# Second feed-forward projection in one core: high weights against high and low activations in one 512-column product

## Chip, core and metric

The kernel runs on one core of one Trainium2 chip. The metric is the device time of one execution in microseconds (us); lower is better. One execution was also taken by the profiler, and all rows below come from that one.

## What is computed

Two transformer-like blocks, one after the other, on 256 tokens of 1024 features, in float32. Among their parts stand eight gated feed-forward blocks. Each adds half of its result to the residual `x`:

```python
def swiglu_ffn(h, w_in, w_out):
    gate, up = jnp.split(h @ w_in, 2, axis=-1)
    return (jax.nn.silu(gate) * up) @ w_out

x = x + 0.5 * swiglu_ffn(rms_norm(x, ffn1_norm[i]), ffn1_w_in[i], ffn1_w_out[i])
```

`w_in` is 1024 x 5632 and `w_out` 2816 x 1024. Between the feed-forward blocks stand the mixers: a recurrent one (rwkv), a gated chunk mixer (gmlp), two cross attentions, a linear recurrence (hgrn) and a dilated attention (dil). All their projections use the same machinery.

## The kernel before, in words

**Products.** Activations are kept transposed, features on the 128 partitions and the 256 tokens (`T`) along the row. A weight matrix comes as "slabs": 128 output features by 8 chunks of 128 input features (512 KB) or, for `w_out`, by 11 chunks (`WIDE`, 704 KB). TensorE rounds its operands in the fast float32r mode, so each operand is split in two: high part and low part. For each chunk three products are added in one bank of PSUM: high weights by high activations, high weights by low activations, low weights by high activations (L470, L475, L476 in `pe_stage`). Each is a weight load of 128 columns and a matmul of 256 columns.

**The ring.** Slabs pass through a ring of 4 slots (`raw`, `hi`, `lo`). SyncE issues the DMA into `raw`; ScalarE rounds it into `hi` (`act_hi`, L339); VectorE subtracts and gives `lo` (`dve_lo`, L347); TensorE uses it and counts `slab_used`. Each step waits on a counting semaphore of the step before.

**A feed-forward block.** The first projection runs over 22 pairs of slabs, gate and up; ScalarE and VectorE make the activation and split it into `Ah` and `Al` (22 chunks of 256 tokens each). The second projection runs over 8 output tiles (`NC`), each of 2 slabs of 11 chunks, so 66 matmuls a tile and 528 a block. Its tiles alternate between banks 0 and 2, and fill the left 256 of the 512 columns of a bank. Blocks are called ffn0 to ffn7 below. In the first round of the ring one of the 528 is issued as two, of 192 and 64 columns (L473, `parted`); several other stages do this too.

**The residual.** After a tile VectorE adds the bank, times 0.5, to the row block of `X` (L623 in `dve_resid`) and counts `banks_freed`. ScalarE then makes the next norm's high part `Hh` (L561) and the square (L565), VectorE the low part `Hl` (L569) and the sum of squares (L579); both then go on with the two slabs that take the freed slots. In ScalarE's and VectorE's queues this order is fixed by the program.

**The joint to the next stage.** Where the next stage starts from `X`, TensorE begins it with chunks 0 to 6 of its first two slabs (42 matmuls, L451 to L453), which need only tiles 0 to 6, then multiplies the sum of squares by a matrix of ones (L645), then takes chunk 7. Two feed-forward blocks, the first and the fourth, are followed by a part that needs the whole norm first (`UNSPLIT`: the rwkv mixer and the norm between the two blocks); there TensorE issues products of constants (L406) to fill the time. After the last block four DMAs on SyncE's queue store `X` (L3050).

Of the kernel before, what the change touches and what calls it, by code (L numbers as in the profile page):

```python
# [24 lines left out]
F32R = mybir.dt.float32r  # L25
I32 = mybir.dt.int32
ALU = mybir.AluOpType
# [3 lines left out]
P = 128  # L31
T = 256
# [186 lines left out]
class Resources:  # L219


    def __init__(self, nc, ctx, io, counts):
        self.nc, self.io = nc, io

        def sb(name, shape, dt=F32):
            return ctx.enter_context(nc.sbuf_tensor(name, shape, dt))

        def sem(name):
            return ctx.enter_context(nc.semaphore(name))


        self.raw = sb("raw", [P, RING, WIDE * P])
        self.hi = sb("hi", [P, RING, WIDE * P], F32R)
        self.lo = sb("lo", [P, RING, WIDE * P], F32R)
        self.X = sb("X", [P, NC, T])
        self.R = sb("R", [P, T])
        self.STD = sb("STD", [P, T])
        self.SQSUM = sb("SQSUM", [P, T])
        self.SQ = sb("SQ", [P, 2, T])
        self.vec = sb("vec", [P, N_COLS])  # L240
        self.cols = sb("cols", [P, ONE_HOT + 15])
        self.masks = sb("masks", [P, len(MASKS), P])
        self.sel = sb("sel", [P, NC * 16])
        self.base = -(-nc.sbuf_base // 64) * 64
        self.room = nc.sbuf_usable_end - self.base
        self.arena = sb("arena", [P, (self.room - 128) // 4])
        self.limit = self.room - 128


        self.Hh = self.at("Hh", 0, [P, NC, T], F32R)  # L250
        self.Hl = self.at("Hl", 8 * KB, [P, NC, T], F32R)
        self.memk = self.at("memk", 16 * KB, [P, NC, T])
        self.memv = self.at("memv", 24 * KB, [P, 2, D])
        self.Kh = self.at("Kh", 16 * KB, [P, NC, T], F32R)
        self.Kl = self.at("Kl", 24 * KB, [P, NC, T], F32R)
        self.RKV = self.at("RKV", 84 * KB, [P, T])
        self.gate = self.at("gate", 32 * KB, [P, 2, T])
        self.sgate = self.at("sgate", 34 * KB, [P, 2, T])
        self.up = self.at("up", 36 * KB, [P, 2, T])
        self.act32 = self.at("act32", 38 * KB, [P, 2, T])  # L260
        self.A0 = 40 * KB
        self.Ah = self.at("Ah", self.A0, [P, FC, T], F32R)
        self.Al = self.at("Al", self.A0 + 22 * KB, [P, FC, T], F32R)

        self.bank = [ctx.enter_context(nc.psum_tensor(f"bank{b}", [P, 512], F32)) for b in range(8)]

        self.ident, self.ones, self.head_ones = self.mask("identity"), self.mask("ones"), self.mask("head_ones")


        self.landed = [sem(f"slab_landed{q}") for q in range(RING)]  # L270
        self.hi_ready = sem("hi_ready")
        self.lo_ready = sem("lo_ready")
        self.slab_used = sem("slab_used")
        self.banks_freed = sem("banks_freed")
        self.h_hi, self.h_lo = sem("h_hi_ready"), sem("h_lo_ready")
        self.kv_hi, self.kv_lo = sem("kv_hi_ready"), sem("kv_lo_ready")
        self.sq_ready, self.sq_added = sem("square_ready"), sem("square_added")
        self.ss_ready, self.std_ready, self.rstd_ready = sem("sumsq_ready"), sem("std_ready"), sem("rstd_ready")
        self.gate_scaled, self.silu_done = sem("gate_scaled"), sem("silu_done")
        self.a_ready, self.ah_ready, self.al_ready = sem("a_ready"), sem("ah_ready"), sem("al_ready")  # L280
        self.gelu_done = sem("gelu_done")
        self.proj_act = sem("projection_activated")
        self.loaded = sem("small_loads")
        self.masks_loaded = sem("masks_loaded")
        self.x_loaded = [sem(f"x_half{h}_loaded") for h in range(2)]
        self.mem_loaded = [sem(f"mem_half{h}_loaded") for h in range(2)]
        self.x_scaled = sem("x_scaled")
        self.mixer_loads = sem("mixer_loads")
        self.mixer_stores = sem("mixer_stores")
        self.pair_loaded = [sem(f"pair_loaded{q}") for q in range(2)]  # L290
        self.out_stored = sem("out_stored")
        self.pe_done = Steps(sem("mixer_products"), counts.setdefault("mixer_products", {}))
        self.act_done = Steps(sem("mixer_activations"), counts.setdefault("mixer_activations", {}))
        self.dve_done = Steps(sem("mixer_vectors"), counts.setdefault("mixer_vectors", {}))
        self.pool_done = Steps(sem("mixer_pool"), counts.setdefault("mixer_pool", {}))

        self.loads_before = 0
# [20 lines left out]
class Shared:  # L318
# [113 lines left out]
    def pe_stage(self, pe, st, moving, ready, between=None, after_first=None, late=False, rest=False, chunks_first=False, pair=False):  # L432
# [83 lines left out]
        else:  # L516
            body(0, parted=True)
            with pe.Fori(1, st.iters) as i:
                body(i)

    def pe_first_stage(self, pe, st, late=False, pair=False):

        self.split_n["pe"] += NC
        self.pe_stage_h(pe, st, lambda: self.norm(pe, "pe"), late, pair=pair)
# [84 lines left out]
            if gain != "mix_norm0":  # L609
                act.preload_act_table(ACT.Sqrt)  # L610

    def dve_resid(self, dve, st, coef, gain, keys=False):

        k, split = self.k, gain not in UNSPLIT
        late = st.per_tile == 1

        def prepare(c):
            dve.wait_ge(k.banks_freed, RING + st.base + (c + 1) * st.per_tile)
            self.prep(dve, "dve", k.X, gain, c, split)
        for c in range(NC):  # L620
            s = st.base + c * st.per_tile
            dve.wait_ge(k.slab_used, s + st.per_tile)
            dve.scalar_tensor_tensor(k.X[:, c, :], k.bank[s % RING][:, :T], coef, k.X[:, c, :],  # L623
                                     ALU.mult, ALU.add).then_inc(k.banks_freed, st.per_tile)
            if gain and late and c:
                prepare(c - 1)
            if gain and (c == NC - 1 or not late):
                prepare(c)
            if keys and c:
                self.keys_lo(dve, c - 1)  # L630
            for kg in range(st.per_tile):
                w = st.width if s + kg + RING < st.base + st.slabs else st.ahead
                self.dve_lo(dve, s + kg + RING, (s + kg) % RING, w)
        if gain:
            self.prepped("dve", split)
# [33 lines left out]
class FeedForward:  # L669
# [7 lines left out]
    def pe(self, pe):  # L677
        sh, k = self.sh, self.k
        if self.n == 0:
            pe.wait_ge(k.x_loaded[0], 16)  # L680
            sh.pe_keep_awake(pe, 5, k.X[:, 0, :P], k.X[:, 1, :])
        sh.pe_first_stage(pe, self.st_in, late=self.n == 0)
        done = 2 + FC * self.n
        sh.pe_stage(pe, self.st_out,
                    lambda kg, kc: (k.Ah[:, kg * WIDE + kc, :], k.Al[:, kg * WIDE + kc, :]),
                    lambda kg, kc: pe.wait_ge(k.al_ready, done + WIDE * kg + kc + 1))

    def act(self, act):
        sh, k, st = self.sh, self.k, self.st_in
# [20 lines left out]
    def dve(self, dve):  # L710
# [7 lines left out]
        def body(i, ahead):  # L718
            for j in range(2):
                m, s = 2 * i + j, st.base + RING * i + 2 * j  # L720
                g = FC * self.n + m
                dve.wait_ge(k.slab_used, s + 1)
                dve.wait_ge(k.silu_done, g + 1)
                dve.tensor_tensor(k.gate[:, j, :], k.bank[2 * j][:, :T], k.R[:], ALU.mult).then_inc(k.gate_scaled, 1)  # L724
                sh.dve_lo(dve, s + RING, 2 * j, ahead)
                dve.wait_ge(k.slab_used, s + 2)
                dve.wait_ge(k.a_ready, g + 1)
                dve.tensor_tensor(k.up[:, j, :], k.bank[2 * j + 1][:, :T], k.R[:], ALU.mult).then_inc(k.banks_freed, 2)
                dve.wait_ge(k.silu_done, g + 3)
                dve.wait_ge(k.banks_freed, RING + s + 2)  # L730
                dve.wait_ge(k.al_ready, g + 1)
                dve.tensor_tensor(k.act32[:, j, :], k.sgate[:, j, :], k.up[:, j, :], ALU.mult).then_inc(k.a_ready, 1)  # L732
                sh.dve_lo(dve, s + 1 + RING, 2 * j + 1, ahead)
                dve.wait_ge(k.ah_ready, g + 1)
                dve.wait_ge(k.a_ready, g + 3)
                dve.tensor_tensor(k.Al[:, bass.ds(m, 1), :].rearrange("p a t -> p (a t)"), k.act32[:, j, :],
                                  k.Ah[:, bass.ds(m, 1), :].rearrange("p a t -> p (a t)").bitcast(F32),
                                  ALU.subtract).then_inc(k.al_ready, 1)
        run(dve, st, body)
        sh.dve_resid(dve, self.st_out, 0.5, self.next_gain, self.keys_next)  # L740


class Memory:
# [2471 lines left out]
```

## Time and profile before

| | us |
|---|---|
| median of 3 runs | 2582.8 |
| lowest, highest run | 2577.11, 2590.47 |
| span of the profiled execution | 2575.4 |
| TensorE busy in it | 2501.2 |
| VectorE, ScalarE busy | 1745.3, 1318.1 |

A busy time is the sum of the stretches in which an engine has an instruction running. Matmuls overlap in their pipeline, so one that lasts 276 ns does not cost 276 ns: what it costs is the distance between the start of one and the start of the next. The profile gives weight loads a row of their own (PEld). "bank<-Ah,lo" reads: into a bank, from the moving operand `Ah` and the weights `lo`.

### The profile page before, as it was taken

How to read it: one execution, taken by the hardware profiler on the slowest of the kernel's cores; microseconds unless marked ns; L12 is line 12 of the kernel's file. 1: busy time of each engine (PE TensorE's matmuls, PEld its weight loads, DVE VectorE, ACT ScalarE, POOL GpSimd, SP SyncE). 2: the span in 40 equal slices, each digit the busy share in tenths (PEclk: the TensorE clock that was granted, in tenths of full speed). 3: DMA queues.
4: the chain of work that ended last, by engine and by line, in shares of the span. 5: the costliest groups of instructions: out<-in, count | busy, mean ns of one | idle time of the engine just before them, and what ended most of it. 6: DMA issues, size and time to landing. Idle time of an engine off the chain costs nothing.

```text
span 2575.4 us, 60687 instructions
## 1 busy us (share of the span) xinstructions
PE 2501.2 (97%) x23366; PEld 2432.5 (94%) x23366; DVE 1745.3 (68%) x2868; ACT 1318.1 (51%) x1998; POOL 79.0 (3%) x122
## 2 busy tenths in 40 slices
PE   8998998999999999999999999899999999999999
PEld 7997877989999999989999999899999999999999
DVE  5757677567757667767757756967667666666774
ACT  5544544455545555545545547455555455555552
POOL 0000442000000000000000000000000000000000
PEclk9999999999999999999999999999999999999999
DMA  5663301435655655445654655235655665553564
GB/s 198 203 215 133 100 11 43 148 125 182 209 184 183 219 200 176 157 138 181 209 174 155 209 174 195 84 115 195 206 173 200 204 177 153 161 160 105 192 211 138
DMA packets 119681, 424.89 MB, mean 165 GB/s; under 512 B 16657, under 2 KB 24420, under 8 KB 119268
## 3 DMA queue, kind: packets, MB, share of 16 engines
q1 hardware_dynamic: 111328, 410.73, 47.6%
q10 hardware_dynamic: 8196, 11.96, 2.4%
q8 instruction: 112, 1.84, 0.3%
q14 instruction: 45, 0.37, 0.0%
HBM read 421.51 MB, written 1.12 MB: 164 GB/s over the span
## 4 chain that ended last, share of the span: by engine, by line
PE 89%; DVE 5%; ACT 3%; issue 2%; POOL 1%; DMA 0%; ACTq 0%; SPq 0%; DVEq 0%; POOLq 0%
PE bank L476 21%; PE bank L470 21%; PE bank L475 21%; PE bank L396 5%; PE bank L398 4%; PE bank L397 4%; PE bank L2327 1%; ACT hi L339 1%; PE bank L451 1%; PE bank L452 1%; PE bank L453 1%; DVE lo L347 1%; PE bank L1730 1%; PE bank L1703 1%; PE bank L1715 1%
## 5 line engine op out<-in xcount | busy, mean ns | idle before, releaser
L347 DVE TENSOR_TENSOR lo<-raw,hi 128x1024 fp32r<-128x1024 f32 (+1 forms) x728 | 935.0, 1292 | 380.6 <-ACT hi L339 378.8
L339 ACT ACTIVATE hi<-raw 128x1024 fp32r<-128x1024 f32 (+1 forms) x728 | 782.6, 1106 | 297.1 <-PE bank L398 170.6
L470 PE MATMUL bank<-Hh,hi 128*128 128x256 f32 x3056 | 845.5, 277 | 4.6 <-DVE lo L347 4.4
L476 PE MATMUL bank<-Hh,lo 128*128 128x256 f32 x3056 | 845.9, 277 | 0.0
L475 PE MATMUL bank<-Hl,hi 128*128 128x256 f32 x3042 | 840.8, 276 | 0.0
L470 PEld LDWEIGHTS bank<-Hh,hi 128*128 128x128 f32 x3056 | 574.5, 188 | 6.2 <-DVE lo L347 5.6
L476 PEld LDWEIGHTS bank<-Hh,lo 128*128 128x128 f32 x3056 | 574.5, 188 | 0.0
L475 PEld LDWEIGHTS bank<-Hl,hi 128*128 128x128 f32 x3042 | 572.2, 188 | 0.0
L476 PE MATMUL bank<-Ah,lo 128*128 128x256 f32 x1408 | 389.3, 277 | 0.0
L470 PE MATMUL bank<-Ah,hi 128*128 128x256 f32 x1408 | 388.6, 276 | 0.0
L475 PE MATMUL bank<-Al,hi 128*128 128x256 f32 x1400 | 386.4, 276 | 0.0
L470 PEld LDWEIGHTS bank<-Ah,hi 128*128 128x128 f32 x1408 | 264.3, 188 | 0.0
L476 PEld LDWEIGHTS bank<-Ah,lo 128*128 128x128 f32 x1408 | 264.3, 188 | 0.0
L475 PEld LDWEIGHTS bank<-Al,hi 128*128 128x128 f32 x1400 | 262.8, 188 | 0.0
L701 ACT ACTIVATE sgate<-gate 128x256 f32<-128x256 f32 x176 | 73.5, 418 | 232.2 <-DVE gate L724 232.2
L705 ACT ACTIVATE Ah<-act 128x256 f32 (+1 forms) x176 | 73.7, 419 | 209.1 <-DVE act L732 209.1
L623 DVE SCALAR_TENSOR_TENSOR X<-bank,X 128x256 f32<-128x256 f32 x112 | 47.4, 424 | 170.8 <-PE bank L476 163.1
L396 PE MATMUL bank<-Hh,hi 128*128 128x256 f32 x528 | 151.9, 288 | 0.0
L561 ACT ACTIVATE Hh<-X,vec 128x256 fp32r<-128x256 f32 x104 | 51.9, 503 | 193.6 <-DVE X L623 190.6
L398 PE MATMUL bank<-Hh,lo 128*128 128x256 f32 x528 | 147.7, 280 | 0.0
L397 PE MATMUL bank<-Hl,hi 128*128 128x256 f32 x528 | 147.7, 280 | 0.0
L396 PE MATMUL bank<-Kh,hi 128*128 128x256 f32 x384 | 112.3, 292 | 0.0
(429 smaller groups left out, 4038.8 us busy)
## 6 DMA issues: line engine op xcount, KB each, us to landing
raw<-in_w SPq DMA_DIRECT2D x600, 512.0 KB, 3.4
raw<-in_w SPq DMA_DIRECT2D x128, 704.0 KB, 4.5
dB<-dil_bias ACTq DMA_DIRECT2D x16, 384.0 KB, 10.4
X<-in_x SPq DMA_DIRECT2D x2, 512.0 KB, 5.3
mem_x<-in_mem ACTq DMA_DIRECT2D x2, 512.0 KB, 3.2
gWS<-in_ws ACTq DMA_DIRECT2D x1, 1024.0 KB
gBS<-in_bs ACTq DMA_DIRECT2D x1, 1024.0 KB
out_x<-X SPq DMA_DIRECT2D x4, 256.0 KB, 2.6
```

The costliest lines, as they stand in the source:

```text
L339: act.activation(k.hi[:, q, :w], k.raw[:, q, :w], ACT.Copy).then_inc(k.hi_ready, 1)
L347: dve.tensor_tensor(k.lo[:, q, :w], k.raw[:, q, :w], k.hi[:, q, :w].bitcast(F32), ALU.subtract).then_inc(k.lo_ready, 1)
L396: pe.matmul(out, wh, xh, start=first and kc == 0, stop=False)
L397: pe.matmul(out, wh, xl, start=False, stop=False)
L398: mm = pe.matmul(out, wl, xh, start=False, stop=last)
L470: pe.matmul(out, wh, xh, start=first, stop=False)
L475: pe.matmul(out, wh, xl, start=False, stop=False)
L476: mm = pe.matmul(out, wl, xh, start=False, stop=last)
L561: eng.activation(k.Hh[:, c, :], src[:, c, :], ACT.Copy, scale=k.v1(gain, c)).then_inc(k.h_hi, 1)
L623: dve.scalar_tensor_tensor(k.X[:, c, :], k.bank[s % RING][:, :T], coef, k.X[:, c, :], ALU.mult, ALU.add).then_inc(k.banks_freed, st.per_tile)
L701: act.activation(k.sgate[:, j, :], k.gate[:, j, :], ACT.Silu).then_inc(k.silu_done, 1)
L705: act.activation(k.Ah[:, bass.ds(m, 1), :].rearrange("p a t -> p (a t)"), k.act32[:, j, :], ACT.Copy).then_inc(k.ah_ready, 1)
```

## The change

A new `pe_out_merged` takes the place of `pe_stage` for the second projection of all eight feed-forward blocks. `Ah` and `Al` become two halves of one tile `A`, so that chunk f of both can be addressed as one moving operand of 2 x 256 columns, 22 KB apart in a partition. The high weights of a chunk are loaded once and meet all 512 columns, with the result in a full bank: left half weights by high activations, right half weights by low activations. The low weights then meet `Ah` alone and add to the left half. So a chunk has 2 weight loads and 2 matmuls (512 and 256 columns) in place of 3 and 3 (256 columns each); in the last chunk of a tile the 256-column matmul comes first. There is no `parted` matmul. The waits for the activations stand in the first round only. VectorE adds the two halves of the bank to `X` one after the other, with a semaphore of its own between the two.

```diff
-        self.Ah = self.at("Ah", self.A0, [P, FC, T], F32R)
-        self.Al = self.at("Al", self.A0 + 22 * KB, [P, FC, T], F32R)
+        self.A = self.at("A", self.A0, [P, 2, FC, T], F32R)
+        self.Ah, self.Al = self.A[:, 0, :, :], self.A[:, 1, :, :]
...
+    def pe_out_merged(self, pe, st, done):
+        k = self.k
+        def body(i, wait=False):
+            for q in range(RING):
+                s, kg = st.base + RING * i + q, q % 2
+                pe.wait_ge(k.lo_ready, s + 1)
+                if kg == 0:
+                    pe.wait_ge(k.banks_freed, s + 1)
+                out = k.bank[q - kg]
+                for kc in range(WIDE):
+                    if wait and q < 2:
+                        pe.wait_ge(k.al_ready, done + WIDE * kg + kc + 1)
+                    f = WIDE * kg + kc
+                    wh, wl = (w[:, q, kc * P:(kc + 1) * P] for w in (k.hi, k.lo))
+                    first, last = f == 0, f == FC - 1
+                    if last:
+                        pe.matmul(out[:, :T], wl, k.Ah[:, f, :], start=False, stop=False)
+                    mm = pe.matmul(out[:], wh, k.A[:, :, f, :], start=first, stop=last)
+                    if not last:
+                        mm = pe.matmul(out[:, :T], wl, k.Ah[:, f, :], start=False, stop=False)
+                mm.then_inc(k.slab_used, 1)
+        body(0, wait=True)
+        with pe.Fori(1, st.iters) as i:
+            body(i)
...
             dve.wait_ge(k.slab_used, s + st.per_tile)
+            if half_of is not None:
+                dve.scalar_tensor_tensor(k.X[:, c, :], k.bank[s % RING][:, T:], coef, k.X[:, c, :],
+                                         ALU.mult, ALU.add).then_inc(k.x_half_added, 1)
+                dve.wait_ge(k.x_half_added, NC * half_of + c + 1)
             dve.scalar_tensor_tensor(k.X[:, c, :], k.bank[s % RING][:, :T], coef, k.X[:, c, :],
                                      ALU.mult, ALU.add).then_inc(k.banks_freed, st.per_tile)
...
-        sh.pe_stage(pe, self.st_out,
-                    lambda kg, kc: (k.Ah[:, kg * WIDE + kc, :], k.Al[:, kg * WIDE + kc, :]),
-                    lambda kg, kc: pe.wait_ge(k.al_ready, done + WIDE * kg + kc + 1))
+        sh.pe_out_merged(pe, self.st_out, done)
...
-        sh.dve_resid(dve, self.st_out, 0.5, self.next_gain, self.keys_next)
+        sh.dve_resid(dve, self.st_out, 0.5, self.next_gain, self.keys_next, half_of=self.n)
```

## Rows read from the trace of the kernel before

**Rows 1.** The page: busy time of TensorE, and the chain's shares by engine.
```profile
PE 2501.2 (97%) x23366; PEld 2432.5 (94%) x23366; DVE 1745.3 (68%) x2868; ACT 1318.1 (51%) x1998; POOL 79.0 (3%) x122
PE 89%; DVE 5%; ACT 3%; issue 2%; POOL 1%; DMA 0%; ACTq 0%; SPq 0%; DVEq 0%; POOLq 0%
```

**Rows 2.** Busy time by stretch: length, each engine's busy time (instructions), clock, DMA share, GB/s.
```profile
711.95:771.95 60.00, 60.00 (x531) 60.00 (x531) 34.16 (x40) 25.89 (x32) 0.00 (x0) 1.00 0.53 180
sum 479.97, PE 479.97 PEld 479.86 DVE 262.79 ACT 200.09 POOL 0.00; mean PE 60.00 PEld 59.98 DVE 32.85 ACT 25.01 POOL 0.00
```

**Rows 3.** Order of time, TensorE, end of ffn1's second projection: start, length, engine, line.
```profile
771.16 0.28 PE L476 MATMUL bank<-Ah,lo 128*128 128x256 f32 x1
771.28 0.28 PE L470 MATMUL bank<-Ah,hi 128*128 128x256 f32 x1
771.39 0.28 PE L475 MATMUL bank<-Al,hi 128*128 128x256 f32 x1
771.50 0.28 PE L476 MATMUL bank<-Ah,lo 128*128 128x256 f32 x1
771.62 0.28 PE L470 MATMUL bank<-Ah,hi 128*128 128x256 f32 x1
```

**Rows 4.** Order of time, weight loads, same stretch.
```profile
771.28 0.19 PEld L475 LDWEIGHTS bank<-Al,hi 128*128 128x128 f32 x1
771.39 0.19 PEld L476 LDWEIGHTS bank<-Ah,lo 128*128 128x128 f32 x1
```

**Rows 5.** Order of time, weight loads, around the parted product of ffn0.
```profile
155.91 0.30 PEld L473 LDWEIGHTS bank<-Al,hi 128*128 128x128 f32 x2
156.13 0.19 PEld L476 LDWEIGHTS bank<-Ah,lo 128*128 128x128 f32 x1
156.24 0.19 PEld L470 LDWEIGHTS bank<-Ah,hi 128*128 128x128 f32 x1
156.36 0.19 PEld L475 LDWEIGHTS bank<-Al,hi 128*128 128x128 f32 x1
```

**Rows 6.** Order of time, TensorE: plain float32 products of constants after ffn0.
```profile
205.88 4.05 PE L406 MATMUL bank<-masks 128*128 128x256 f32 x18
```

**Rows 7.** Order of time, weight loads around the product of ones (L645) after ffn1.
```profile
776.94 0.19 PEld L451 LDWEIGHTS bank<-Hh,hi 128*128 128x128 f32 x1
777.15 0.19 PEld L452 LDWEIGHTS bank<-Hl,hi 128*128 128x128 f32 x1
777.27 0.19 PEld L453 LDWEIGHTS bank<-Hh,lo 128*128 128x128 f32 x1
```

**Rows 8.** Busy time by stretch, TensorE alone: rwkv's output projection; products under a halved clock.
```profile
503.43:526.12 22.69, 22.69 (x196) 1.00 0.54 181
1358.90:1361.01 2.11, 2.11 (x11) 0.50 0.00 0
```

**Rows 9.** Order of time, VectorE: two last tiles of ffn1; two dependent steps (L728, L732) later.
```profile
764.75 0.42 DVE L623 SCALAR_TENSOR_TENSOR X<-bank,X 128x256 f32<-128x256 f32 x1 [1.74 <-PE bank L476]
767.01 2.36 DVE L347 TENSOR_TENSOR lo<-raw,hi 128x1024 fp32r<-128x1024 f32 x2 [0.37 <-ACT hi L339]
772.23 0.42 DVE L623 SCALAR_TENSOR_TENSOR X<-bank,X 128x256 f32<-128x256 f32 x1 [2.86 <-PE bank L476]
773.30 0.49 DVE L569 SCALAR_TENSOR_TENSOR Hl<-X,vec,Hh 128x256 fp32r<-128x256 f32 x1 [0.65 <-ACT Hh L561]
773.70 0.42 DVE L579 TENSOR_TENSOR SQSUM<-SQSUM,SQ 128x256 f32<-128x256 f32 x1
782.93 0.42 DVE L728 TENSOR_TENSOR up<-bank,R 128x256 f32<-128x256 f32 x1
783.38 0.43 DVE L732 TENSOR_TENSOR act<-sgate,up 128x256 f32<-128x256 f32 x1
```

**Rows 10.** Order of time, TensorE: product of ones after ffn1 and after ffn3.
```profile
776.72 0.59 PE L645 MATMUL bank<-SQSUM,masks 128*128 128x256 f32 x2
1349.48 0.70 PE L645 MATMUL bank<-SQSUM,masks 128*128 128x256 f32 x2 [1.55 <-DVE SQSUM L579]
```

**Rows 11.** Waits of the weight loads, 2072 to 2090 us: total, times, longest.
```profile
PEld bank L396 <- DVE lo L347: 0.6, 1, 0.6
```

**Rows 12.** End of the program: VectorE's last addition, the stores on SyncE's queue.
```profile
2570.35 0.42 DVE L623 SCALAR_TENSOR_TENSOR X<-bank,X 128x256 f32<-128x256 f32 x1 [7.06 <-PE bank L476]
2570.80 1.82 SPq L3050 DMA_DIRECT2D out_x<-X  x4
```

More of the change, by code:

```diff
@@ L287, in __init__ @@
         self.x_scaled = sem("x_scaled")
+        self.x_half_added = sem("x_half_added")
         self.mixer_loads = sem("mixer_loads")
@@ L610, in act_resid, with dve_resid @@
                 act.preload_act_table(ACT.Sqrt)
-    def dve_resid(self, dve, st, coef, gain, keys=False):
+    def dve_resid(self, dve, st, coef, gain, keys=False, half_of=None):
         k, split = self.k, gain not in UNSPLIT
```

## The prediction, made before the changed kernel had run

> **What bounds the kernel now.** I read the page first: TensorE is busy 97% of the span and holds 89% of the chain that ends last [rows 1]. So only what changes the pace of TensorE, or makes it wait, can move the time. Next the busy time by stretch, over the second projections: the eight stretches of 60 us hold TensorE busy throughout at the full clock (2.4 GHz), 480 us in all, 19% of the span, with some 531 matmuls each [rows 2]. VectorE is busy 34 of 60 us there, ScalarE 26, the DMAs half [rows 2]. The stage waits for nobody; its length is the number of products times their distance. Last, the order of time inside the stage: matmuls start at 771.16, .28, .39, .50 and .62, so 0.1133 us apart, and a chunk of three (from 771.28 to 771.62) takes 0.340 us [rows 3]. A stage has 8 x 22 = 176 chunks, 176 x 0.340 = 59.8 us, which is the stretch.
>
> **What sets the 0.1133 us.** This decides the case, because the change removes one product of three and no column: a chunk streams 768 columns before and after. If the distance belongs to the columns, merging brings nothing; if part belongs to each product, or to its weight load, that part is saved. Two readings of the trace:
> - The next weight load starts when the current matmul does (771.28 and 771.39 in both views) [rows 3, 4]: one set is loaded behind the running one. Around the parted product the matmuls have 192, 64 and 256 columns. The loads there start at 155.91, a second one inside that row, then 156.13, .24 and .36 [rows 5]. Two loads after 155.91 it is 156.13, 0.11 each; then 0.11 again, although 64 columns could have streamed in a quarter of the time that 256 need. So a product has a floor near 0.110 us, set by its load, whatever its columns.
> - Without that floor, columns cost less than 0.1133 per 256. Under the halved clock (1.2 GHz) 10 distances fill the 2.11 us from 1358.90 to 1361.01 [rows 8], 0.211 to 0.215 us for 256 columns; that is one column per clock (256 / 1.2 = 213 ns) and no surcharge. At the full clock the plain float32 constants, which pass 512 column slots each, take (4.05 - 0.38) / 17 = 0.216 us, with 0.38 us the length of the last [rows 6]; the second half of the ones product lasts from 776.94 to 777.15, 0.21 [rows 7].
>
> The Trainium skill ("TensorE: Matmul & The Clock Gate", section "LDWEIGHTS") puts a load at its columns over 1.2 GHz, 107 ns for 128: the trace's floor of 0.11 us agrees. The same page (section "Back-to-back issue gap") gives columns / 2.4 + 2.5 ns for a warm matmul alone, so 109 ns for 256 and 216 ns for 512. By that alone the chunk would go from 327.5 to 325 ns, worth 3.5 us over 1408 chunks; the trace has 340 now, so the loads do count here.
>
> **The change part by part.**
> - The 512-column product. No row has one in float32r. Bounds: 0.2133 us, twice 256 columns at twice the clock of the slow row [rows 8], and 0.2267 us, two of today's distances [rows 3]. Its neighbour is the plain float32 product with as many column slots and its load equally hidden; I take 0.2155 us [rows 6, 7]. The load of the low weights (0.11 us) goes on behind it and costs nothing: its cover is the 512-column product; uncovered it would be 0.11 us a chunk.
> - The 256-column product after it. Its end waits for the load of the next chunk's high weights, begun when it starts. Bounds: 0.110 us (the floor) [rows 5] and 0.122 us (156.24 to 156.36, the widest distance after a disturbed product) [rows 5]. Where a product paced by its columns comes before, the next one takes 777.15 to 777.27 = 0.12 [rows 7], and a whole stage can stay there: rwkv's output projection has 192 distances in 22.69 us, 0.118 each [rows 8]. In the merged order every short product follows a long one, so I take 0.118.
> - Sum for a chunk: 0.2155 + 0.118 = 0.3335 us against 0.340; saved 0.0065 us, times 176 x 8 = 1408 chunks: 9.2 us. At the bounds: 0.3233 (saves 23 us) and 0.3487 (loses 12 us).
> - The parted product goes, once a stage. It is a fourth load where three stood, 0.11 us, and a few slower distances behind it [rows 5]: 0.12 x 8 = 1.0 us saved.
> - VectorE's second addition, 64 times. It costs 0.45 us, the distance of two dependent steps of this size (782.93 to 783.38) [rows 9], 3.6 us a stage on an engine with 26 of 60 us free [rows 2]. Behind it in VectorE's queue stand `Hl`, the sum of squares and two `lo` slabs, and ScalarE waits for `X` before `Hh`, the square and two `hi` slabs; SyncE's next raw DMAs wait for `lo`. Inside the stage the two slabs are ready at 767.01 + 2.36 = 769.4, and TensorE takes them up when the next tile is over, at about 772: 2.6 us of cover against 0.45 us more work and tiles 0.15 us shorter. Nothing.
> - The same at the joints. Where 42 products of the next stage stand between (after ffn1, 2, 4, 5 and 6) the last sum of squares is ready at 774.1 and wanted at 776.72 [rows 9, 10]: 2.6 us of cover, nothing. Behind the ones product all goes by TensorE's own time. After ffn6 TensorE already waits 0.6 us for a `lo` slab that VectorE makes late [rows 11]: 0 to 0.45 us, I take 0.4. After ffn0 and ffn3 TensorE waits 1.55 us for the sum of squares, straight behind the addition (the row is that of ffn3; the same wait of 1.55 us stands in the trace after ffn0) [rows 10]: 0.45 us each. At the end the stores follow the last addition at once, 2570.35 + 0.42 to 2570.80 [rows 12]: 0.45 us. Together 1.75 us lost.
> - Waits for `al_ready` dropped from later rounds, the tile `A`, fewer instructions: no idle time stands before these products, so nothing to gain.
>
> Sum: -9.2 - 1.0 + 1.75 = -8.4 us. The profiled execution spanned 2575.4 us, so its span would be 2567.0. The median of the runs is 7.4 us above that span, part of it what lies around a span and part scatter (the runs spread over 13 us). Applied to the median: 2582.8 - 8.4 = 2574.4 us.
>
> **The rivals.**
> 1. The short product keeps its present distance. Today's stage holds 0.1133 in spite of everything [rows 3]. Then 0.2155 + 0.1133 = 0.3288, saving 15.8 us: -15.8 - 1.0 + 1.75 = -15, 2567.7 us. Against it: each time a column-paced product came before, the next took 0.12 [rows 7].
> 2. The cost belongs to the columns, or to a fresh start of each product, in float32r at the full clock: the 512-column product takes 0.2267 [rows 3] and the short one 0.118. Chunk 0.3447, 0.0047 more than now, times 1408 = +6.6; with the parted product gone and the joints +7.4: 2590.2 us. This is the case on the slower side. It sits in the second projections on TensorE, and it decides from the chunk's length: above 0.340 - 0.75 / 1408 = 0.3395 us the change loses. For it: no row has a product of over 256 columns in float32r, and none of its products at the full clock goes faster than 0.1133 in a long row [rows 3, 8]. Against it: the two column-paced rows at either clock show 0 to 2.5 ns of surcharge [rows 6, 8].
> 3. Nothing is saved because a product of 512 columns behaves as two: chunk 0.340, only the joints and the parted product count, +0.75: 2583.5 us.
> 4. Much faster: a long product overlaps its neighbours and costs no more than one of today's, 0.1133 us [rows 3]. The chunk would be 0.2267, 0.1133 saved, times 1408 = 160 us: 2423 us. The rows speak against it: 512 column slots take 0.216 us at the full clock [rows 6]. The Trainium skill (same page, section "Back-to-back issue gap") gives 131 ns for sustained products of 512 columns, which with its 81 ns for short ones would also be a large gain; the 0.216 us row disagrees with it, so the chance is small.
>
> Beside these, what the next stages do: their pace is 0.113 or 0.118 depending on how they were entered [rows 3, 8]. 42 first products at the slower pace after five blocks would be 1 us, and a stage that flips may give or take 2 us.
>
> **How the numbers follow.** Forecast (saving 3 to 12 us) 0.50; rival 1 0.22; rival 2 0.13; rival 3 0.14; rival 4 0.01. A measurement tells about 0.5% from no change, 12.9 us. Rival 1 is beyond this more often than not, and the forecast with good luck: faster 0.27. Rival 2 reaches it only near its upper bound (+12): slower 0.08. Within 0.5%: 0.65. The range for 8 in 10 goes from 2564 (rival 1 with 4 us of scatter) to 2590 (rival 2).
>
> **What would show it.** In the order of time of a second projection: the 512-column product followed by the next after 0.2155 us, the 256-column one after 0.118, no idle time between; each stretch 58.6 to 58.8 us in place of 59.9, TensorE still at the full clock. L623 twice per tile, 0.45 apart. The wait before the ones product after ffn0 and ffn3 at 2.0 us in place of 1.55, none after the others. Wrong would be: a chunk at or above 0.340, a load that only starts after the 512-column product, a `lo` slab that TensorE waits for inside the stage, or a halved clock in new places behind the longer waits.

## The result, and the profile after

| | before | changed |
|---|---|---|
| median (us) | 2582.49 (7 runs) | 2599.04 (7 runs) |
| lowest, highest | 2577.11, 2590.65 | 2596.46, 2603.75 |
| ratio, 95% interval | | 1.0068 (1.0049 to 1.0088) |
| span of the profiled execution | 2575.4 | 2597.3 |

The changed kernel is slower by 0.68%, 17.6 us by the ratio, with 13 to 23 us as the interval. The forecast was 8.4 us faster, and the range ended at 2590.

TensorE is again busy 97% of the span; there is no new idle time to find. The page of the changed kernel, its first line, the chain by engine and the two groups of the new products:

```profile
PE 2525.2 (97%) x21950; PEld 2391.1 (92%) x21950; DVE 1773.5 (68%) x2932; ACT 1319.2 (51%) x1998; POOL 78.9 (3%) x122
...
PE 90%; DVE 5%; ACT 2%; issue 2%; POOL 1%; DMA 0%; ACTq 0%; SPq 0%; DVEq 0%; POOLq 0%
...
L541 PE MATMUL bank<-A,hi 128*128 128x512 f32 x1408 | 493.6, 397 | 0.0
L543 PE MATMUL bank<-A,lo 128*128 128x256 f32 x1344 | 377.8, 281 | 0.0
```

There are 1416 matmuls fewer and TensorE is busy 24 us longer [rows 1]. The place is the second projection. The same busy time by stretch as in [rows 2], for ffn1, from its first product to the first product of the next stage (columns: stretch, length, busy time and instructions of PE, PEld, DVE, ACT, POOL, clock, DMA share, GB/s):

```profile
714.37:776.49 62.12, 62.12 (x354) 53.99 (x353) 37.19 (x47) 25.92 (x32) 0.00 (x0) 1.00 0.52 174
```

62.12 us in place of 59.97 (from 711.99 to 771.96 in the trace of before), at the full clock, without a gap. And inside it, order of time on TensorE, to be held against [rows 3]:

```profile
730.60 0.40 PE L541 MATMUL bank<-A,hi 128*128 128x512 f32 x1
730.83 0.28 PE L543 MATMUL bank<-A,lo 128*128 128x256 f32 x1
730.95 0.40 PE L541 MATMUL bank<-A,hi 128*128 128x512 f32 x1
731.19 0.28 PE L543 MATMUL bank<-A,lo 128*128 128x256 f32 x1
731.30 0.40 PE L541 MATMUL bank<-A,hi 128*128 128x512 f32 x1
```

The long product holds TensorE from 730.95 to 731.19, 0.235 us; the short one to 731.30, 0.118. A chunk takes 0.353 us (62.12 / 176) where it took 0.340; the digits that the two decimals of the rows do not give are means over the stage. The weight loads, which answer to [rows 4]:

```profile
730.84 0.19 PEld L541 LDWEIGHTS bank<-A,hi 128*128 128x128 f32 x1
730.95 0.19 PEld L543 LDWEIGHTS bank<-A,lo 128*128 128x128 f32 x1
731.19 0.19 PEld L541 LDWEIGHTS bank<-A,hi 128*128 128x128 f32 x1
```

Each still starts with the product ahead of it (730.95 and 731.19 in both views). A load with its product takes 0.1117 us where nothing else limits it (measured below), so by this estimate the low weights are in place 0.12 us before the long product gives way. TensorE does not wait for this load. Whether a load that runs behind the long product slows it down is a question for the last rows of products below.

The joints. VectorE's two additions at the end of ffn1, and TensorE's wait ahead of the ones product after ffn3, to be held against [rows 9, 10], and the end of the program, against [rows 12]:

```profile
776.69 0.42 DVE L652 SCALAR_TENSOR_TENSOR X<-bank,X 128x256 f32<-128x256 f32 x1 [2.62 <-PE bank L541]
777.22 0.42 DVE L655 SCALAR_TENSOR_TENSOR X<-bank,X 128x256 f32<-128x256 f32 x1
...
1360.67 0.79 PE L677 MATMUL bank<-SQSUM,masks 128*128 128x256 f32 x1 [2.01 <-DVE SQSUM L607]
...
2592.21 0.42 DVE L655 SCALAR_TENSOR_TENSOR X<-bank,X 128x256 f32<-128x256 f32 x1
2592.66 1.82 SPq L3080 DMA_DIRECT2D out_x<-X  x4
```

The second addition starts 0.53 us after the first, and the exposed wait grew by 0.46, from 1.55 to 2.01.

### The profile page after: what moved, and what is told of

The parts are those of the page before. It is cut to its first block, busy times and chain, and to the rows that moved or that the text cites. A ratio compares the mean times of both kernels' runs of the same rounds, so it can differ in the third digit from the quotient of the medians.

```text
span 2597.3 us, 57965 instructions
## 1 busy us (share of the span) xinstructions
PE 2525.2 (97%) x21950; PEld 2391.1 (92%) x21950; DVE 1773.5 (68%) x2932; ACT 1319.2 (51%) x1998; POOL 78.9 (3%) x122
## 4 chain that ended last, share of the span: by engine, by line
PE 90%; DVE 5%; ACT 2%; issue 2%; POOL 1%; DMA 0%; ACTq 0%; SPq 0%; DVEq 0%; POOLq 0%
PE bank L477 15%; PE bank L471 15%; PE bank L476 15%; PE bank L541 13%; PE bank L543 6%; PE bank L397 5%; PE bank L399 4%; PE bank L398 4%; PE bank L2357 1%; ACT hi L340 1%; PE bank L452 1%; PE bank L453 1%; PE bank L454 1%; DVE lo L348 1%; PE bank L1760 1%
## 5 line engine op out<-in xcount | busy, mean ns | idle before, releaser
L541 PE MATMUL bank<-A,hi 128*128 128x512 f32 x1408 | 493.6, 397 | 0.0
L543 PE MATMUL bank<-A,lo 128*128 128x256 f32 x1344 | 377.8, 281 | 0.0
L541 PEld LDWEIGHTS bank<-A,hi 128*128 128x128 f32 x1408 | 260.7, 188 | 59.2
L543 PEld LDWEIGHTS bank<-A,lo 128*128 128x128 f32 x1344 | 252.2, 188 | 2.5
L735 ACT ACTIVATE A<-act 128x256 f32 (+1 forms) x176 | 73.7, 419 | 197.5 <-DVE act L762 197.5
L652 DVE SCALAR_TENSOR_TENSOR X<-bank,X 128x256 f32<-128x256 f32 x64 | 27.1, 424 | 131.8 <-PE bank L541 131.8
L399 PE MATMUL bank<-Kh,lo 128*128 128x256 f32 x384 | 107.4, 280 | 0.0
L398 PE MATMUL bank<-Kl,hi 128*128 128x256 f32 x384 | 107.4, 280 | 0.0
```

The source lines that it names most:

```text
L398: pe.matmul(out, wh, xl, start=False, stop=False)
L399: mm = pe.matmul(out, wl, xh, start=False, stop=last)
L541: mm = pe.matmul(out[:], wh, k.A[:, :, f, :], start=first, stop=last)
L543: mm = pe.matmul(out[:, :T], wl, k.Ah[:, f, :], start=False, stop=False)
L735: act.activation(k.Ah[:, bass.ds(m, 1), :].rearrange("p a t -> p (a t)"), k.act32[:, j, :], ACT.Copy).then_inc(k.ah_ready, 1)
```

## The experiments

Where a ratio is given, it is against the kernel before on the same chip. Two questions: what makes the long product cost 0.235 us, and what sets the pace of the 256-column ones, 0.1133 or 0.118.

### Is it the jump between the two halves?

The chunk's high and low activations side by side, so that the long product reads one run of 512 columns:

```diff
-        self.A = self.at("A", self.A0, [P, 2, FC, T], F32R)
-        self.Ah, self.Al = self.A[:, 0, :, :], self.A[:, 1, :, :]
+        self.A = self.at("A", self.A0, [P, FC, 2, T], F32R)
+        self.Ah, self.Al = self.A[:, :, 0, :], self.A[:, :, 1, :]
...
-                    mm = pe.matmul(out[:], wh, k.A[:, :, f, :], start=first, stop=last)
+                    mm = pe.matmul(out[:], wh, k.A[:, f, :, :], start=first, stop=last)
```

> Edit to the changed kernel: the high and low activations of one chunk lie side by side (tile A as 22 x 2 x 256), so the 512-column product reads one run of 512 columns in place of two runs 22 KB apart. In the changed kernel a chunk takes 0.353 us: 0.235 for the long product, 0.118 for the short. Theory 'columns' (each float32r column has a price of its own, 0.44 to 0.46 ns, however the product is cut): 0.235 and 0.118 stay, a second projection stays at 61.9 us, the time near 2599. Theory 'two runs' (the jump between the two halves costs 0.02 us): the long product falls to 0.2155, a chunk to 0.333, a second projection to 58.7 us, the time to about 2574.

Measured: 2599.7 us, ratio 1.0074 (1.0045 to 1.0103). Order of time on TensorE, inside ffn1's second projection:

```profile
729.90 0.40 PE L541 MATMUL bank<-A,hi 128*128 128x512 f32 x1
730.14 0.28 PE L543 MATMUL bank<-A,lo 128*128 128x256 f32 x1
730.26 0.40 PE L541 MATMUL bank<-A,hi 128*128 128x512 f32 x1
```

From 729.90 to 730.26 it is 0.353 again (mean over the stage). The jump costs nothing; the theory of the two runs falls.

### Is it the long product, or what came with it?

Everything of the change stays (layout, full bank, two additions, order of products), but in 20 of 22 chunks the long product is cut in two:

```diff
-                    mm = pe.matmul(out[:], wh, k.A[:, :, f, :], start=first, stop=last)
+                    if first or last:
+                        mm = pe.matmul(out[:], wh, k.A[:, :, f, :], start=first, stop=last)
+                    else:
+                        mm = pe.matmul(out[:, :T], wh, k.Ah[:, f, :], start=False, stop=False)
+                        mm = pe.matmul(out[:, T:], wh, k.Al[:, f, :], start=False, stop=False)
```

> Edit to the changed kernel: in chunks 1 to 20 of each tile (of 0 to 21) the 512-column product is cut into two of 256 columns into the two halves of the bank; both additions on VectorE stay. Theory 'columns at a slow pace': what is lost comes from the pace that the long products bring (0.118 per 256 columns in place of 0.1133); with three products of 256 the chunk goes back to 0.340 us or stays at 0.353 if the pace once entered holds. At 0.340 a second projection takes 59.9 us and the time is that of the kernel before plus the joints, about 2585; at 0.353 it is 61.9 and 2599. Theory 'the full bank or the second addition costs': the chunk stays above 0.345 also with short products after a fast entry.

Measured: 2581.1 us (10 runs), ratio 1.0002 (0.9985 to 1.0018): no different from the kernel before. Order of time in ffn1 around a long product, and the busy time of the stretch:

```profile
721.82 0.40 PE L542 MATMUL bank<-A,hi 128*128 128x512 f32 x1
722.05 0.28 PE L547 MATMUL bank<-A,lo 128*128 128x256 f32 x1
722.17 0.28 PE L544 MATMUL bank<-A,hi 128*128 128x256 f32 x1
722.29 0.28 PE L545 MATMUL bank<-A,hi 128*128 128x256 f32 x1
722.40 0.28 PE L547 MATMUL bank<-A,lo 128*128 128x256 f32 x1
722.51 0.28 PE L544 MATMUL bank<-A,hi 128*128 128x256 f32 x1
722.63 0.28 PE L545 MATMUL bank<-A,hi 128*128 128x256 f32 x1
```
```profile
706.56:766.78 60.22, 60.22 (x515) 1.00 0.54 178
```

The long product takes 0.23 to 0.235; a few products later the short ones are back at 0.1133 (722.29, .40, .51, .63). That holds for the second to the eighth tile. In the first one, behind its single long product, the short ones stayed at 0.118 to the end of the tile, in the seven blocks that were entered at 0.1133; in ffn6, entered at 0.118, they ran at 0.1133 behind it. So a long product, too, can change the pace of the short ones behind it, either way. With 160 loads and 160 products more than in the changed kernel the stretch is 1.9 us shorter. So the loss comes with the long product, by its own length and by the pace of the short one behind it: the bank, the layout and the second addition together cost no more than the comparison can tell (0.2%, 5 us).

### Does the parted product restore the pace?

The changed kernel with the parted product put back, on the low weights:

```diff
-                    if not last:
+                    if wait and q == RING - 1 and kc == 3:
+                        for cols in (slice(0, T - 64), slice(T - 64, T)):
+                            mm = pe.matmul(out[:, cols], wl, k.Ah[:, f, cols], start=False, stop=False)
+                    elif not last:
                         mm = pe.matmul(out[:, :T], wl, k.Ah[:, f, :], start=False, stop=False)
```

> Edit to the changed kernel: in the first round of the ring, slot 3, chunk 3, the 256-column product with the low weights is issued as 192 and 64 columns, as the kernel before did in this stage. Theory 'the parted product sets the pace': the rest of the stage goes at 0.1133 per 256 columns, 0.2267 for the long product, 0.340 a chunk; a second projection takes 60.0 us, the time is about 2584. Theory 'the long product itself brings the slow pace': 0.353 stays after it, a second projection takes 62.0 us, the time about 2600.

Measured: 2601.7 us, ratio 1.0088 (1.0063 to 1.0112). After the parted product, in ffn1:

```profile
740.15 0.40 PE L541 MATMUL bank<-A,hi 128*128 128x512 f32 x1
740.38 0.28 PE L546 MATMUL bank<-A,lo 128*128 128x256 f32 x1
740.50 0.40 PE L541 MATMUL bank<-A,hi 128*128 128x512 f32 x1
```

Still 0.353 a chunk. The parted product does not help while every chunk holds a long product.

### The products by themselves

The kernel before, with rows of products behind its last one. Nothing else runs then but the stores of the result, and their own results are not used, so the kernel computes what it did. Each kind of row stands twice: behind a plain float32 product (entry S) and behind a product parted into 192 and 64 columns (entry P). "One run" and "two runs" say whether the 512 columns lie in one piece or in two, 22 KB apart. In short:

```diff
+        for n in range(24):
+            pe.matmul(out[:], w(n), both, start=n == 0, stop=n == 23)
...
+        for n in range(24):
+            pe.matmul(out[:], w(n), apart[:, :, n % 22, :], start=n == 0, stop=False)
+            pe.matmul(out[:, :T], w(n, True), k.Ah[:, n % 22, :], start=False, stop=n == 23)
```

> The kernel before, with eight rows of float32r products into a spare bank added on TensorE behind its last product, each row once behind a plain float32 product (entry S) and once behind four 256-column products and a 192 + 64 pair (entry P). Their results are not used. Rows: 48 products of 256 columns; 48 of 128; 24 of 512 in one run; 24 of 512 in two runs 22 KB apart; 24 pairs of 512 in two runs and 256; 24 pairs of 512 in one run and 256; 24 of 512 in two runs, each opening the bank anew; 24 of 384. Theory 'columns': 512 takes 0.227 (P) or 0.235 (S), 384 takes 0.170 or 0.176, 256 takes 0.113 or 0.118, and 128 takes the floor of its weight load, 0.110. Theory 'two runs': 0.2155 for 512 in one run, 0.235 in two. Theory 'adding into PSUM costs': 0.2155 where the bank is opened anew. Theory 'a surcharge per product': 384 takes 0.160 + 0.007 and 512 takes 0.213 + 0.007.

Measured, the mean distance of starts within a row in the trace, without its first two. All are from one execution:

| product | entry S (us) | entry P (us) | ns per column |
|---|---|---|---|
| 128 columns | 0.1117 | 0.1116 | |
| 256 | 0.1178 | 0.1137 | 0.460, 0.444 |
| 384 | 0.1748 | 0.1748 | 0.455 |
| 512, one run | 0.2330 | 0.2333 | 0.456 |
| 512, two runs | 0.2333 | 0.2333 | 0.456 |
| 512, bank opened anew | 0.2334 | 0.2334 | 0.456 |
| pair 512 + 256, two runs | 0.3533 | 0.3531 | 0.460 |

Two of the stretches of 22 distances each, for 512 columns in one run and with the bank opened anew, entry P (columns: stretch, length, TensorE busy, clock, DMA share, GB/s):

```profile
2644.60:2649.73 5.13, 5.13 (x23) 1.00 0.00 0
2675.49:2680.62 5.13, 5.13 (x23) 1.00 0.00 0
```

5.13 / 22 = 0.2332. The changed kernel's chunk of 0.353 stands here with no other engine at work. As causes of the long product's price, traffic of the other engines, the jump, adding into the bank and the entry are all out. 128 columns take 0.1117, close to the floor of 0.110 that the prediction gave the load. At 384 and 512 columns a float32r column costs 0.455 to 0.456 ns, against 0.417 for one clock at 2.4 GHz. "A surcharge per product" falls too: at 384 it would be 0.167, and 0.1748 was measured.

### Whose price is it?

The same, with other shapes and types, each row behind entry P:

```diff
+    row(24, lambda n: out[:64, :512], lambda n: w(n)[:, :64], lambda n: x(n, 512))
+    row(24, lambda n: out[:, :512], lambda n: w(n)[:64, :], lambda n: x(n, 512)[:64, :])
...
+    row(24, lambda n: out[:, :512], lambda n: w(n).bitcast(BF)[:, :128], lambda n: x(n, 512).bitcast(BF)[:, :512])
+    row(24, lambda n: out[:, :512], lambda n: w(n), lambda n: x(n, 128).unsqueeze(1).broadcast_to([P, 4, 128]))
```

> The kernel before, with eleven rows of products added behind its last one, each behind four 256-column float32r products and a 192 + 64 pair; results not used. Rows of float32r unless said: (1) 256 columns, weights of 128 columns; (2) 256, weights of 64 columns; (3) 512, weights of 64 columns; (4) 512 with 64 of 128 rows of partitions; (5) 320; (6) 448; (7) 512, banks in turn; (8) 512 in plain float32; (9) 512 in bfloat16; (10) 256 in bfloat16; (11) 512 read as one block of 128 columns four times. Theory 'price per float32r column': (3) and (7) 0.233, (2) 0.117, (5) 0.146, (6) 0.204, (9) 0.2155. Theory 'the weight load behind it slows the moving columns': with half the load (3) falls to 0.223, (2) to 0.110 or below, and (9) keeps a surcharge. Theory 'reading four bytes a column from the moving tile': (11) still 0.233, (9) 0.2155. Theory 'writing the result': (3) falls, because only 64 partitions are written, and (9) stays at 0.233, because it writes as much. Row (8) 0.431 or more.

Order of time on TensorE; the shape reads weights' rows x columns, then the moving operand. The length covers all products of a row; plain float32 shows two instructions per product, and its row (at 2607.89) holds 12 products:

```profile
2572.71 5.89 PE L3137 MATMUL bank<-A,hi 128*64 128x256 f32 x48
2579.04 5.77 PE L3137 MATMUL bank<-A,hi 128*64 128x512 f32 x24
2585.36 5.86 PE L3137 MATMUL bank<-A,hi 64*128 64x512 f32 x24
2591.87 3.76 PE L3137 MATMUL bank<-A,hi 128*128 128x320 f32 x24
2596.08 5.10 PE L3137 MATMUL bank<-A,hi 128*128 128x448 f32 x24
2601.61 5.84 PE L3137 MATMUL bank<-A,hi 128*128 128x512 f32 x24
2607.89 10.55 PE L3137 MATMUL bank<-A,hi 128*128 128x512 f32 x24
2618.89 5.36 PE L3137 MATMUL bank<-A,hi 128*128 128x512 bf16 x24
2624.70 5.42 PE L3137 MATMUL bank<-A,hi 128*128 128x256 bf16 x48
2630.57 5.84 PE L3137 MATMUL bank<-A,hi 128*128 128x512 f32 x24
```

The distances behind them, means without the first two:

| row | us |
|---|---|
| float32r, 256 columns, weights of 128 columns | 0.1135 |
| float32r, 256 columns, weights of 64 columns | 0.1188 |
| float32r, 512, weights of 64 columns | 0.2326 |
| float32r, 512, 64 rows | 0.2334 |
| float32r, 320 and 448 | 0.1467, 0.2025 |
| float32r, 512, banks in turn | 0.2333 |
| float32r, 512, the same 128 columns four times | 0.2329 |
| plain float32, 512, per instruction | 0.4292 |
| bfloat16, 512 | 0.2158 |
| bfloat16, 256 | 0.1092 |

bfloat16 takes 0.2158, the price that the prediction gave float32r. Plain float32 has none of the surcharge either: 0.4292 for each of the two instructions, and 1024 clocks at 2.4 GHz, two for each column, are 0.4267. So among the three types the surcharge is float32r's alone, and neither half the load (0.2326 in place of 0.2333), half the rows read, half the rows written nor fewer distinct columns takes it away. From 320 to 512 columns a float32r column costs 0.452 to 0.458 ns.

What in float32r makes it stays open. Every row here loads weights for each product, so none shows the price with no load at all. And the bfloat16 rows differ in the load too: in the trace theirs last 0.098 us, those of float32r 0.188. Against the load as the cause stand the row with half of it and plain float32, whose loads last 0.190 without a surcharge.

The Trainium skill ("TensorE: Matmul & The Clock Gate", section "Back-to-back issue gap") gives columns / 2.4 + 2.5 ns for a warm product by itself, 215.8 and 109.2 ns here: the bfloat16 rows agree to 0.1 ns, the float32r rows are 17 ns above it at 512 columns.

### The pace of the short products

The kernel before with nothing but the parted product taken out of its second projections:

```diff
-            body(0, parted=True)
+            body(0, parted=not whole)
```

> The kernel before with its second projections free of the parted product (528 matmuls a stage in place of 529), nothing else. These stages are entered at the fast pace (0.1133 us). Theory 'the pace is kept from the entry': 0.1133 throughout, a second projection goes from 59.85 to 59.73 us, the time falls by 1 us, less than can be told. Theory 'the parted product is what keeps the stage fast': the stage goes at 0.118, 62.2 us, and the time rises by 19 us to about 2599, that of the changed kernel.

Measured: 2580.2 us (12 runs), ratio 0.9993 (0.9975 to 1.0012). The stretches of ffn1 and ffn5 in the profiled execution:

```profile
715.89:775.73 59.84, 59.84 (x530) 1.00 0.54 182
1844.60:1906.78 62.18, 62.18 (x530) 1.00 0.51 169
```

ffn1 was entered fast and kept 0.1133. ffn5 and ffn6 were entered from first projections that ran at 0.118 in this execution (the expectation took all eight entries for fast), and kept 0.118, 2.3 us more each. So without a parted product all eight stages kept the pace that they were entered with. The parted product is not needed where the entry is fast, and costs the 0.12 us that the prediction gave it (59.73 in place of 59.85 from first to last start).

What the parted product does with a slow entry stands in the trace of the products by themselves, whose first 2579 us are the kernel before. There ffn4 and ffn6 were entered at 0.118. In ffn4 the parted product brought the fast pace. In ffn6 it did not, and the stage took 62.18 us from first to last start, against 59.85 in the kernel before's own trace:

```profile
2022.71:2084.89 62.18, 62.18 (x530) 1.00 0.52 172
```
Over all nine traces, wherever steady products of 256 columns stand on both sides, a parted product turned the slow pace into the fast one 79 times, left it slow 19 times, and never turned fast into slow.

Then the kernel without the parted product, with a plain float32 product ahead of each second projection:

```diff
+        pe.matmul(k.bank[5][:, :T], k.ones, k.mask("identity", 2).rearrange("p a t -> p (a t)"), start=True, stop=True)
         sh.pe_stage(pe, self.st_out,
```

> The kernel before without the parted product in its second projections, and with one plain float32 product of constants (0.43 us) ahead of each, which in other stages of the traces is followed by the slow pace. Three products of 256 columns a chunk as before, no second addition. Theory 'the pace is set by what stood before and holds': 0.118 per product, 0.354 a chunk, a second projection takes 62.2 us, the time is 8 x (2.4 + 0.5) = 23 us above the kernel before, about 2603. Theory 'three products fall back into the fast pace by themselves': 59.9 us a stage, 2584. The first would say that the changed kernel's chunk (0.353) costs what today's three products cost at the slow pace, and that the change loses by giving up the fast one.

Measured: 2596.9 us, ratio 1.0062 (1.0041 to 1.0084). Order of time in ffn1, and the stretches of ffn1 and ffn5:

```profile
739.92 0.28 PE L470 MATMUL bank<-Ah,hi 128*128 128x256 f32 x1
740.04 0.28 PE L475 MATMUL bank<-Al,hi 128*128 128x256 f32 x1
740.16 0.28 PE L476 MATMUL bank<-Ah,lo 128*128 128x256 f32 x1
740.28 0.28 PE L470 MATMUL bank<-Ah,hi 128*128 128x256 f32 x1
```
```profile
709.70:772.07 62.37, 62.37 (x530) 1.00 0.52 173
1843.19:1903.24 60.05, 60.05 (x530) 1.00 0.53 172
```

Five stages, entered fast, went over to the slow pace: 739.92 to 740.28, 0.354 a chunk. ffn5 and ffn6 came in slow, and there the same product brought the fast pace; ffn0 went over to the slow pace too and came back to the fast one behind a wait of 0.68 us. So the plain float32 product toggles the pace rather than sets it, and the forecast of eight slow stages was too simple. With products, loads and columns of the kernel before, the lost pace alone costs as much per chunk (0.354) as the merge (0.353).

## Why the prediction was wrong

**The step that failed** is the first term of the sum, the 512-column product at 0.2155 us. Measured: 0.235 in the kernel, 0.2333 in a row of its own kind. 0.0195 x 1408 = 27 us, which turns the forecast gain of 9 in the chunks into a loss of 18. The other term of the chunk, 0.118 for the short product, was right. Against the kernel before, the long product is 0.008 us dearer than two short ones at the fast pace, and the remaining short one loses the fast pace, 0.005: together the 0.013 a chunk. The price came from a plain float32 row [rows 6] and a half-clock row [rows 8], and both were read as the price of a column slot in general. At the halved clock float32r does pay nothing extra, and at the full clock plain float32 pays nothing extra; the one case that counted, float32r at the full clock in a product of over 256 columns, had no row of its own. The halved row was counted loosely, without harm to the price: from 1358.90 to 1361.11 stand 10 distances, nine of 0.213 to 0.214 and one of 0.287. Three of its starts:

```profile
1359.11 0.41 PE L451 MATMUL bank<-Hh,hi 128*128 128x256 f32 x1
1359.33 0.41 PE L452 MATMUL bank<-Hl,hi 128*128 128x256 f32 x1
1359.54 0.41 PE L453 MATMUL bank<-Hh,lo 128*128 128x256 f32 x1
```

The bound taken for it was wrong as well: twice today's distance, 0.2267, is no upper bound, since 0.1133 is the fast pace of the 256-column product. Twice the slow pace [rows 8], 0.236, was in the rows and would have been right.

**Rival 2** had the mechanism (the cost belongs to the columns) and the side, with 13%. Its price used that same 0.2267: chunk 0.3447 in place of 0.353, +7.4 us in place of about 18. The measured chunk is well above its deciding point of 0.3395. Of the others, rival 1 wanted 0.1133 for the short product behind a long one, rival 3 a chunk of 0.340 and rival 4 0.1133 for the long product; none of these was measured.

**Point by point.**
- The short product after a long one: forecast 0.118, measured 0.118.
- The load hidden behind the long product: right, every load starts with the product ahead of it.
- What sets 0.1133: "a floor set by the load" was half of it. The floor is there (0.1117 for 128 columns), but 256 columns at 0.456 ns are 0.117, above it: at the slow pace the columns account for these products, and with half the load they take no less (0.1188). So the product and the load that were removed per chunk had cost nothing of their own: three short ones at the slow pace take 0.354, the merged chunk 0.353. The fast pace, 0.443 ns a column, is below the price of a column in every longer product, and no run shows what makes it.
- The parted product: 0.12 us a stage where the entry is fast, right. That it can also bring the fast pace back was no part of the sum.
- The second addition inside the stage: hidden, right (the stretch is busy without a gap). At the exposed joints 0.53 us, forecast 0.45: the wait ahead of the ones product went from 1.55 to 2.01 (forecast 2.0).
- After ffn6 the wait for `lo` stayed at 0.6 us, where 0.4 more was forecast.
- The clock: the granted clock is 1.00 in all eight second projections, right. Over the whole execution it is 0.995, in the kernel before 0.992, so the loss does not come from the clock.

**The sum as measured**: 2.15 us for each of eight stretches (62.12 against 59.97, the parted product in it) = 17.2; three exposed joints at 0.5 = 1.5; together 18.7 us, against 17.6 (13 to 23) by the ratio. The profiled executions lie 21.9 us apart. The other 3.2 us are the balance of larger differences in both directions in stages that the change doesn't touch. In the changed kernel's trace the first projections of ffn0 and ffn7 ran at 0.118, in the other at 0.1133; the part between ffn0 and ffn1 was 3.8 us shorter. The last first projection, changed kernel and kernel before:

```profile
2409.70:2529.20 119.50, 119.50 (x1016) 1.00 0.60 194
```
```profile
2394.70:2510.00 115.30, 115.30 (x1016) 1.00 0.60 199
```

4.2 us, with the same instructions. Such a flip happens from one execution to the next: in the trace of the products by themselves, whose part up to 2579 us is the kernel before, the first projections of ffn4 and ffn6 ran at 0.118, and in the kernel before's own trace none did. The stretches of ffn4 in the two:

```profile
1366.56:1486.19 119.63, 119.63 (x1017) 1.00 0.57 190
```
```profile
1365.68:1481.07 115.39, 115.39 (x1018) 1.00 0.58 195
```

So the flip of a first projection is no part of the change's price. That these flips also make the scatter of 13 us between runs of one kernel is likely by their size, but is not shown: most of those executions have no trace.

No version tried beats the kernel before. From the measured prices none of this kind should: at 384 and 512 columns a float32r column costs 0.455 to 0.456 ns, in the 256-column product at its fast pace 0.443.

## What to carry to other kernels

Before merging products, find what a product costs beyond its columns in the very type and clock that it runs in: if three products of n columns already take what their columns cost, fewer and longer ones save nothing. A price carried over from another type or clock is a guess, and twice a measured distance is a bound only if the distance has no faster and slower form. Where one instruction's distance comes in two sizes in a trace, price the new stage at both, since any edit may change which of them it gets.

## What the runs showed that was not expected

- A float32r column costs 0.452 to 0.458 ns at the full clock (320 to 512 columns), a bfloat16 column 0.4215 at 512; at the halved clock 256 float32r columns take their 0.213 us and nothing more.
- 256-column float32r products with 128-column loads have two steady paces, 0.1133 and 0.118 us. The pace can last for a whole stage and pass into the next. A plain float32 product changed it either way, and so did a 512-column product (first tiles of the three-product run); a parted product changed it only from slow to fast. With 64-column loads the fast pace did not appear (0.1188, one row).
- Over a first projection of 1015 products the slow pace is worth 4.2 us, over a second projection 2.3 us.
